# A recurrent scan's TensorE program as a loop of one pair a turn, with fixed operand buffers filled by DMA, in one core's layer kernel

## The reference, cut to what matters

```python
def rwkv_scan(s0, r, w, a, b, k, v):
    def step(s, inp):
        r_t, w_t, a_t, b_t, k_t, v_t = inp
        sa = jnp.einsum('bdhvk,bdhk->bdhv', s, a_t)
        s = s * w_t[..., None, :] + sa[..., None] * b_t[..., None, :] + v_t[..., None] * k_t[..., None, :]
        return s, jnp.einsum('bdhvk,bdhk->bdhv', s, r_t)
    s_fin, y = lax.scan(step, s0, (r, w, a, b, k, v))
    return y, s_fin
```

## Time and profile before

| what | value |
|---|---|
| median of three runs | 2658.68 us |
| the profiled execution, its own time | 2655.93 us |
| its span, first to last instruction | 2654.0 us |
| TensorE matmul busy | 2427.3 us (91%) |
| VectorE, ScalarE, GpSimd busy | 1352.5, 699.4, 656.4 us |
| mean granted TensorE clock | 0.972 |
| instruction DMA queue, whole span | 163 packets, 2.67 MB |
| tile stage, about | 545 to 1015 us |
| scan, about | 1016 to 1341 us |

### The profile page before, as it was taken

One profiled execution on the slowest core, in us unless ns is written; L12 is line 12 of the kernel. 1 busy time (PEld: TensorE's weight loads), 2 busy tenths in 40 slices (PEclk: granted clock), 3 DMA queues, 4 the chain that ended last, 5 costly groups with the idle time before them and its releaser, 6 DMA issues.

```text
span 2654.0 us, 50075 instructions
## 1 busy us (share of the span) xinstructions
PE 2427.3 (91%) x21498; PEld 1997.5 (75%) x21498; DVE 1352.5 (51%) x2117; ACT 699.4 (26%) x1159; POOL 656.4 (25%) x283
## 2 busy tenths in 40 slices
PE   2799999999999997777788999899999999999997
PEld 2677778787888786777754578788888888888886
DVE  7665656528697866444453332543433334333335
ACT  3272644735655431222210000310001000010002
POOL 0220120111111111111100035253344344444431
PEclk9899999999999998989988999899999999999999
DMA  6313111022566767223222320011110111111112
GB/s 241 99 51 109 49 60 59 27 107 70 168 178 185 205 173 238 83 88 100 72 90 99 107 96 32 16 42 38 41 41 32 41 40 40 33 40 41 36 37 87
DMA packets 176353, 225.09 MB, mean 85 GB/s; under 512 B 100898, under 2 KB 135842, under 8 KB 175266
## 3 DMA queue, kind: packets, MB, share of 16 engines
q1 hardware_dynamic: 176162, 222.19, 26.4%
HBM read 163.30 MB, written 57.02 MB: 83 GB/s over the span
## 4 chain that ended last, share of the span: by engine, by line
PE 79%; DVE 7%; issue 6%; ACT 2%; DMA 2%; SPq 2%; POOL 1%; DVEq 0%; ACTq 0%; POOLq 0%
PE PS L808 18%; PE PS L810 18%; PE PS L809 18%; PE PS L1249 5%; PE PS L917 3%; PE PS L931 2%; PE PS L1059 2%; SPq L658 2%; PE PS L889 2%; DVE buffer L1911 1%; DVE buffer L1910 1%; PE PS L903 1%; PE PS L960 1%; PE PS L891 1%; PE PS L1110 1%
## 5 line engine op out<-in xcount | busy, mean ns | idle before, releaser
L808 PE MATMUL PS<-buffer,buffer 128*128 128x512 f32 (+1 forms) x2784 | 1006.0, 361 | 19.8 <-POOL buffer L2167 8.3
L810 PE MATMUL PS<-buffer,buffer 128*128 128x512 f32 (+1 forms) x2784 | 997.4, 358 | 0.0
L809 PE MATMUL PS<-buffer,buffer 128*128 128x512 f32 (+1 forms) x2784 | 997.2, 358 | 0.0
L808 PEld LDWEIGHTS PS<-buffer,buffer 128*128 128x128 f32 x2784 | 526.7, 189 | 113.8 <-issue 17.9
L810 PEld LDWEIGHTS PS<-buffer,buffer 128*128 128x128 f32 x2784 | 526.8, 189 | 83.2
L809 PEld LDWEIGHTS PS<-buffer,buffer 128*128 128x128 f32 x2784 | 526.9, 189 | 81.9 <-issue 1.0
L2176 POOL TENSOR_TENSOR buffer<-buffer,buffer 128x1024 fp32r<-128x1024 f32 x76 | 183.9, 2420 | 856.5 <-PE PS L810 528.0
L2123 DVE SCALAR_TENSOR_TENSOR buffer<-PS,buffer,buffer 128x512 f32<-128x512 f32 (+1 forms) x264 | 158.4, 656 | 154.8 <-PE PS L810 154.8
L2177 POOL TENSOR_TENSOR buffer<-buffer,buffer 128x1024 fp32r<-128x1024 f32 x76 | 193.4, 2545 | 6.0
L2099 DVE TENSOR_SCALAR buffer<-buffer,buffer 128x1281 f32<-128x1281 f32 x22 | 34.5, 1568 | 291.7 <-ACT buffer L1680 291.7
L1680 ACT ACTIVATE buffer<-PS 128x512 f32<-128x512 f32 (+1 forms) x66 | 30.0, 530 | 513.6 <-PE PS L810 513.6
(11 more groups left out here) (209 smaller groups left out, 2916.2 us busy)
## 6 DMA issues: line engine op xcount, KB each, us to landing
buffer<-in_w_up SPq DMA_DIRECT2D x44, 512.0 KB, 3.4
buffer<-in_w_in SPq DMA_DIRECT2D x42, 512.0 KB, 5.1
ops_kept<-buffer SPq DMA_DIRECT2D x40, 512.0 KB, 5.7
buffer<-ops_kept SPq DMA_DIRECT2D x40, 512.0 KB, 4.3
buffer<-in_w_ada SPq DMA_DIRECT2D x32, 512.0 KB, 7.0
buffer<-in_w_down SPq DMA_DIRECT2D x22, 512.0 KB, 3.4
buffer<-in_x SPq DMA_DIRECT2D x20, 512.0 KB, 10.1
gates_kept<-buffer SPq DMA_DIRECT2D x16, 640.0 KB, 5.7
```

Source lines behind the costliest of these rows:

```text
L808: mm(out, w_hi, x_hi, start=start, stop=False)
L809: mm(out, w_hi, x_lo, start=False, stop=False)
L810: return mm(out, w_lo, x_hi, start=False, stop=stop)
```

## The change

TensorE's scan becomes a first turn written out and a loop of 19 turns, whose operands lie at the same addresses in every turn and whose wait values are in registers. So no buffer takes turns: the grams, Vt, Q, S and the loaded operands have one copy each. A pair's operands come by 22 DMAs instead of four: FX (A and R), FBK (B and K) and FV (values) with two each, and DX with 16, since the solved blocks now go by DMA straight into the zeroed DX. ScalarE copies FX to FY, GpSimd's `expand` goes, and VectorE's `read_out` moves to the tile stage, where the R operand is multiplied by r from RS, loaded by four DMAs per unit (`load_reads`). The units begin three tiles later, the last batch is solved in eight pieces within the scan and stored by 16 DMAs at pair 9, and r, k and v come back by three DMAs of 2.5 MB after pairs 3, 5 and 7. The new state is stored after the scan. Semaphores are merged (`tiles_moved`).

```diff
-        UNIT_SLOT = [6 + 2 * u for u in range(NG_UNITS)]
+        UNIT_SLOT = [9 + 2 * u for u in range(NG_UNITS)]
-        SOLVE_SLOT = [(12 + 4 * b, 14 + 4 * b) if b < NBATCH - 1 else (28, 29) for b in range(NBATCH)]
+        SOLVE_SLOT = [(15 + 4 * b, 17 + 4 * b) for b in range(NBATCH - 1)]
...
+            def load_reads(u):
...
+                for c in range(4):
+                    sp.dma_start(RS[c // 2][:, c % 2 * NP:(c % 2 + 1) * NP, :], kept[:, 0:4, at + c * C:at + (c + 1) * C]).then_inc(rs_in, 16)
...
-            def load_pair(i):
...
+            def load_grams(i):
+
+                if i >= 1:
+                    sp.wait_ge(fy_ready, i)
+                    sp.wait_ge(gk_done, i)
                 sp.wait_ge(ops_out, 128 * (i // 4 + 1))
                 for d in range(2):
+                    sp.dma_start(FX[:, 2 * d:2 * d + 2].rearrange("p a j t -> p (a j t)"),
+                                 dram["ops_kept"][d, :, chunk_at(d, i) // C, 0:2 * NP * C]).then_inc(fx_in, 16)
+
+            def load_keys_b(i):
+
+                if i >= 1:
+                    sp.wait_ge(bk_done, i)
...
+            def load_values(i):
+
+                if i >= 1:
+                    sp.wait_ge(vt_done, i)
+                for d in range(2):
+                    sp.dma_start(FV[:, d * NP:(d + 1) * NP, :], kept[:, 8:12, chunk_at(d, i):chunk_at(d, i) + C]).then_inc(fv_in, 16)
+
+            def load_solved(i):
+
+                if i >= 1:
+                    sp.wait_ge(q_done, i)
+                else:
+                    sp.wait_ge(cleared, 4)
+                sp.wait_ge(solved_out, 256 * (i // 4 + 1))
+                for d in range(2):
                     n = chunk_at(d, i) // C
...
+                    for q in range(4):
+                        dst = DX[HB * q:HB * q + HB, :, d * NP:(d + 1) * NP, HB * (q % 2):HB * (q % 2) + HB]
+                        for kind in range(2):
+                            sp.dma_start(dst[:, kind], dram["solved_kept"][d, HB * q:HB * q + HB, kind, n * NP * HB:(n + 1) * NP * HB]
+                                         .rearrange("s (j t) -> s j t", t=HB)).then_inc(dx_in, 16)
...
+                if t - 1 in UNIT_SLOT:
+                    load_reads((t - 1 - UNIT_SLOT[0]) // 2)
...
+            load_solved(0)
             for i in range(1, NC):
-                load_pair(i)
-                if i == 2:
-                    store_solved(NBATCH - 1)
+                load_grams(i)
+                load_keys_b(i)
+                load_values(i)
+                load_solved(i)
+                if i == 1:
...
+                if i in (3, 5, 7):
+                    n = (i - 3) // 2
+                    sp.dma_start(rkv[:, 4 * n:4 * n + 4, :], kept[:, 4 * n:4 * n + 4, :]).then_inc(state_in, 16)
+                if i == 9:
+                    store_solved(NBATCH - 1)
...
+            def hold(*waits):
+
+                pe.wait_ge(consts_in, 48)
+                for sem, value in waits:
+                    pe.wait_ge(sem, value)
+
+            def turn(i, after, twice, loads, blocks, first=False):
+
+                if not first:
+                    hold((rh_out, i), (q_out, i))
+                    products(6, Q, RH).then_inc(u_done, 1)
+                hold((fx_in, loads), (fbk_in, loads))
+                gram(0, 2).then_inc(gb_done, 1)
+                if not first:
+                    hold((u_out, i), (ys_done, i))
+                    outputs_of_tokens().then_inc(y_done, 1)
+                    state_update().then_inc(st_done, 1)
+                    hold((vt_out, i))
+                gram(1, 4).then_inc(gk_done, 1)
+                if not first:
+                    hold((y_out, twice), (fy_ready, i))
+                to_tokens(Y_BANK, 0, lambda j: FBK[:, 2 * (j // NP), j % NP, :])
+                to_tokens(Y_BANK, NP * C, lambda j: FBK[:, 2 * (j // NP) + 1, j % NP, :]).then_inc(bk_done, 1)
+                hold((far_out, after), (s_ready, after), (dx_in, blocks))
                 products(7, GB[:, 0], DX[:, 1]).then_inc(lz_done, 1)
+                hold((gk_out, after), (fv_in, loads))
+                to_tokens(TURN_BANK, 0, lambda j: FV[:, j, :]).then_inc(vt_done, 1)
+                hold((lz_ready, after))
                 products(7, Z, DX[:, 0]).then_inc(q_done, 1)
+                hold((gb_out, after), (fy_ready, after))
+                rhs_of_state().then_inc(rh_begun, 1)
+                hold((vt_out, after))
+                rhs_of_values(EVEN)
+                hold((rh_begun, after))
+                rhs_of_values(ODD).then_inc(rh_done, 1)
+                hold((bk_out, after))
+                outputs_of_state().then_inc(ys_done, 1)
...
+            with ExitStack() as counts:
+                after, twice, loads, blocks = (counts.enter_context(pe.register(n)) for n in ("after", "twice", "loads", "blocks"))
+                with pe.Fori(1, NC) as i:
+                    pe.reg_add(after, i, 1)
+                    pe.reg_add(twice, i, i)
+                    pe.reg_mul(loads, after, 32)
+                    pe.reg_mul(blocks, after, 256)
+                    turn(i, after, twice, loads, blocks)
...
+            def keep_grams(i):
+                act.wait_ge(fx_in, 32 * (i + 1))
+                if i >= 1:
+                    act.wait_ge(ys_done, i)
+                act.activation(FY, FX, ACT.Copy).then_inc(fy_ready, 1)
...
             def dve_pair(i):
 
-                mask_gram(i, 0, 2, GB, gram_far)
+                dve.wait_ge(gb_done, i + 1)
+                mask_gram(2, GB, gram_far, 0, far_out)
                 if i >= 1:
+                    dve_y(i - 1)
                     dve_state(i - 1)
+                mask_gram(2, GB, gram_far, 1, gb_out)
+                dve.wait_ge(gk_done, i + 1)
+                mask_gram(4, GK, gram_mask, 0, None)
+                mask_gram(4, GK, gram_mask, 1, gk_out)
                 dve.wait_ge(lz_done, i + 1)
...
             for i in range(NC):
                 dve_pair(i)
+                if i < 8:
+                    if i == 0:
+                        begin_solve(NBATCH - 1)
+                    solve(ROWS_BACK[4 * i:4 * i + 4])
+                    if i == 7:
+                        end_solve()
```

More of the change, by code:

```diff
@@ L696, in _ @@
                     load_blocks((t - 3 - UNIT_SLOT[0]) // 4)
[L697 to L706 removed]
+                if t == 24:
+                    sp.wait_ge(conv_done, 12)
+                    load_grams(0)
+                    load_keys_b(0)
+                    load_values(0)
                 if t == 29:
@@ L1103, in seq_state, with state_update @@
-            def seq_state(n):
-                out = two_banks(0)
-                for lhs, rhs, first in ((Bt, U, True), (Kt, Vt[:, n % 2], False)):
+                for j, k in zip(ODD, EVEN):
+                    one(k)
+                    ins = one(j)
+                return ins
+            def state_update():
+                for lhs, rhs, first in ((Bt, U, True), (Kt, Vt, False)):
                     for j in range(2 * NP):
@@ L1109, in seq_state @@
                             f, t = halves(j, h)
-                            ins = mm(out[f, j % 2, j // 2, :], lhs[t, j, :], rhs[t, j, :], start=first and j < 2, stop=not first,
+                            ins = mm(at_bank(STATE_BANK, j)[f], lhs[t, j, :], rhs[t, j, :], start=first and j < 2, stop=not first,
                                      skip_group_check=True)
-                ins.then_inc(st_done, 1)
-            def seq_rhs(n):
-                p = n % 2
-                out = two_banks(0)
-                def of_state(j):
+                return ins
@@ L1127, in of_values, with rhs_of_values @@
+            def rhs_of_values(group):
+                for j in group:
                     for h in range(2):
                         _, t = halves(j, h)
-                        ins = mm(out[t, j % 2, j // 2, :], GK[t, 0, j, :], Vt[t, p, j, :], start=False, stop=True,
-                                 skip_group_check=True)
-                    return ins
-                for j in range(2 * NP):
-                    ins = of_state(j)
-                ins.then_inc(odd_begun, 1)
-                for j in EVEN:
-                    of_values(j)
@@ L1896, in unit_keys, with begin_solve, solve @@
                 V.link(tt(SG[:, 0], SG[:, 0], KS, ALU.mult))
-                tt(SG[:, 0], SG[:, 0], PX2, ALU.mult).then_inc(keys_ready, 1)
-            def solve(b, half):
-                if half == 0:
-                    dve.wait_ge(m_in, 16 * (b + 1))
-                    if b >= 1:
-                        dve.wait_ge(solved_out, 256 * b)
-                    V.link(dve.memset(X32, 0.0))
-                    V.link(dve.memset(X32.rearrange("p s t -> p (s t)")[:, 0:HB * HB:HB + 1], 1.0))
-                for p in (range(HB - 1, HB // 2, -1) if half == 0 else range(HB // 2, 0, -1)):
+                V.step(tt(SG[:, 0], SG[:, 0], PX2, ALU.mult))
+                dve.wait_ge(rs_in, 64 * (u + 1))
+                for n in range(2):
```

(14 more changed lines are left out.)

370 lines of the change are left out of this document (139 added, 231 removed).

## The result

The changed kernel takes 2642.77 us (median of five runs, 2641.05 to 2647.58) where the kernel before, in the same session, took 2658.68 (2656.91 to 2662.21). The ratio is 0.9944, with a 95% interval of 0.9929 to 0.9958: 15.9 us or 0.6% faster. The forecast was 2669 and slower. The time lies inside the range and on the other side of no change.

What follows compares the result with a forecast made beforehand. Instruction fetching was taken to bound the scan, and a VectorE-SyncE ring as long as TensorE's four tiles the tile stage. 16.2+17.5-23.4 = +10.3 us on 2655.93 gives 2666.2, with the median 2.75 above: 2669, range 2635 to 2705.

Steps and rivals of the forecast that it cites:

- The order of the rings: Scan turn: SyncE's ring of DX loads decides at 13.0 us, VectorE's follows at 12.1, TensorE's work is 10.4.
- A DX DMA behind another: Scan, SyncE's queue: issuing each solved-block DMA takes 0.465 us, with ends 0.37 and 0.57.
- the ones behind the 2.5 MB loads and the store at pair 9: Scan: small loads held up behind three large loads cost +15 us, behind the store +10.
- its cover: Scan's start: VectorE's solve covered the old start; now SyncE's queue takes its place, 31.1 us instead of 13.6.
- Rival C: Scan: the loop fetches instructions anyway, turn 16.2 us, 2712 us in all; chance 0.08.
- rival D: Scan: a DX DMA costs 0.57 us like one of 256 runs, turn 14.8, 2697 us in all; chance 0.19.
- A turn: 13.3: Scan: a loop turn takes 13.3 us instead of 15.6, set by SyncE's DX loads; whole scan -23.4 us.
- The clock's 0.3: Scan turn: TensorE's waits sometimes drop the clock to 1.2 GHz, raising the turn from 13.0 to 13.3 us.
- Tile stage: +16.2: Tile stage: read-row loads (3.9 us) and VectorE's additions (1.5) lengthen each of three rings by 5.4 us.
- keeps the ring's form: Tile stage: moving all slots by three tiles leaves the VectorE and SyncE ring unchanged, three rings between four solves: 16.2 us.
- Start: +17.5: Scan's start: from the last tile's store to the first product takes 31.1 us instead of 13.6, through SyncE's stores and loads.
- Rival B: Scan: a DX DMA issues in 0.37 us, VectorE's 12.1 us ring decides, not slower, 2644 us; chance 0.28.

Runs made afterwards that it cites:

- e1: Changed kernel with the nineteen turns of TensorE's scan written out again, constants in place of registers: 2719.58 us, 1.0215 to the kernel before.
- e10: Changed kernel without the tile stage's loads of read rows, its multiplications by them cut to one element (part of the computation left out): 2631.44 us.
- e5: Changed kernel with eight of each turn's sixteen solved-block DMAs issued earlier, right after the first products: 2636.11 us, 0.9912 to the kernel before.
- e14: Changed kernel with ScalarE issuing the last two batches' stores, solved blocks loaded by kind, stored rows reloaded in twelve pieces: 2595.82 us.

## Why the prediction was wrong

**What held.** The fetching ends with the loop (6 packets for 74); e1 shows that without the loop the change is a loss. The order of the rings is right: SyncE's decides, VectorE's is next (12.1 forecast, 11.68 measured once the first is loosened), TensorE's work is shorter. A DX DMA behind another costs 0.465 (measured 0.467), the ones behind the 2.5 MB loads and the store at pair 9 cost +15 and +10 (measured, as what the turns 4 to 9 and 10 to 11 take above 12.2 us each: 18.2 and 11.0), and the start loses its cover to SyncE. Rival C is refuted by the trace, rival D by 0.467. The Trainium skill, page "Runtime: NRT & Kernel Launch", section "Instruction fetch mechanics", has a taken branch beyond two 16 KiB pages fetch again, and gives TensorE a larger store; this loop's six packets in nineteen turns speak for the second, and e1's 75 against preferring the code written out.

**What failed** is the size of three terms, all on one side, in a sum of +10.3 whose parts were each above it. By the profiled executions it was -13.7 (without the rest's -0.8).

1. *A turn: 13.3, measured 12.2.* Of the 1.1, the landing is 1.0: the step took 2.8 from L658, whose DMAs are stores of 64 KB, for loads of 16 KB, which land in 1.8. The clock's 0.3 was not lost either: in the steady turns it is 1.00 (2.4 GHz) though TensorE waits 1.4 us in each. The issues to the start of the sixteenth took 7.04, the forecast had 7.2. Against that, the way from the first product to the first issue was 3.24 us and not 2.9: it goes over Z and the second product, and the values' two loads, 0.92 and not 1.5, are done before. (The forecast's parts of this ring also add up to 12.9, not 13.0, and VectorE's to 12.0, not 12.1.) Over nineteen turns the term is 21 us, more than the whole forecast. Elsewhere the scan was slower than forecast (turns 1 to 3 by 4.3, where the first loads of DX took 9.2 us to issue and 2.8 to land; the large loads by 3.2, the store by 1.0, the end by 1.3), so 277.2 instead of 288.2.
2. *Tile stage: +16.2, measured +8.0.* For the two additions e10 shows 1.4, 4.8 and 5.0 us a ring, 11.2 in all, where the step had 5.4 three times; in the first profile the three rings together grew by 8.7. The size was nearly right in two rings and failed in the first. What failed there is "keeps the ring's form": TensorE's own work in the first stretch rose from 64.6 to 67.4 us and hides most of them. That is the slack, which the forecast had put at 1 us in every ring. As a whole the stage is as long as before without the additions (67.6, 64.9 and 62.6 us, 195.1 in sum, against 65.5, 65.0 and 64.7, 195.2).
3. *Start: +17.5, measured +12.7.* The same landing again (1.0), the solve done 13.5 us after the last keys instead of 15.3, and the last tile's store 10.3 us after them instead of 8.3.

**Rival B** gave 2644, the time that came, by another way: a DX DMA at 0.37 and VectorE as the bound. Its price is refuted (0.467) and its bound too (e5 shows what happens when VectorE does decide). That its number fits is worth nothing for the mechanism; the chance of "faster" should have come from errors of the terms. With 19 turns in the sum, an error of half a us a turn is as large as the result, and the forecast gave itself "errors of some 10" in all.

## What to carry to other kernels

When a program written out is streamed in, the first question for a loop is not what fetching costs but what paces the turn without it. Here that is one engine issuing 22 small DMAs, sixteen of them at 0.47 us each and no cheaper when cut in half: count DMAs per turn and per issuing engine, take those out of the ring whose buffer is free earlier, cut large transfers that small ones queue behind, and give the stores to an engine that idles, where they cost something still (0.6 to 1.3 us a turn for four here). A landing is to be taken from a transfer of the same direction and size; a difference of 1 us in a ring that turns nineteen times decides the sign of such a change.

## What the runs showed of the hardware

- In the scan the time to issue a DMA did not fall with its size: 0.467 us with 128 runs (16 KB), 0.475 with 64 (8 KB), one behind another.
- The written-out program cost more than its waits: beside 49 us of "issue" in e1's scan, the clock of the group norm behind it was 0.75 instead of 0.80, with the same program there. What lowered it wasn't tried.
- ScalarE issues a store of 64 KB in 0.9 us under the scan's start (5.47 for six) and in 0.4 to 0.75 later, no faster than SyncE (the median is 0.67 us on both); what it has is the idle time.
- Issuing on two engines at once was not free: eight loads of 16 KB on SyncE took 4.7 to 5.1 us beside four of ScalarE's stores and 3.8 without, in the same profile (e14). Whether the issuing or the traffic of the stores delays them isn't shown.
